# The front of a three-block network on one core: order of the loads, modulation products in four column quarters, and four of 31 convolution taps on TensorE

## The chip, the cores and the metric

The kernel runs on one core of a Trainium2 chip. The metric is the device time of one execution in microseconds; the time before is the median of three runs, 2841.48 us (2841.01 to 2846.5).

## What is computed

The reference chains two transformer-like layers over 512 latent and 256 context tokens of width 1024 and a third block over the latent tokens. Only the beginning matters here: the modulation vectors, the first norm, and the "conformer" convolution of the first layer.

```python
sc, scc = silu(c), silu(c_ctx)                       # 1024 each
mod_lat = sc @ ada_w[i] + ada_b[i]                   # i = 0, 1; 6 x 1024 columns each
mod_ctx = scc @ ada_w[i] + ada_b[i]                  # split in sh1, sc1, g1, sh2, sc2, g2
a = rmsnorm(h, norm1_g[0]) * (1 + sc1) + sh1         # 768 tokens x 1024
def conformer_conv(h, ...):
    u = h @ w_pw1 + b_pw1                            # 1024 -> 2048
    a, g = split(u, 2)
    v = a * sigmoid(g)
    v = dwconv(v, w_dw, b_dw)                        # depthwise, 31 taps over the tokens
    v = silu(layernorm(v, ln_g, ln_b))
    return v @ w_pw2 + b_pw2
h = h + g1 * conformer_conv(a, ...)
```

Everything is float32. `ada_w` is 2 x 1024 x 6144, some 50 MB, and is read once.

## The kernel before

Activations lie transposed: channels on the 128 partitions, tokens along the free axis, so a [1024, 768] activation is eight tiles k of 128 x 768. Each engine has its own hand-written program; they meet by counting semaphores, and each engine executes its own in order.

**Weights.** A 1024 x 128 piece of a weight matrix is a chunk. SyncE loads it into `raw` (two slots), ScalarE rounds it into `w_hi` (`high`, L520), GpSimd computes the rest `w_lo` = raw - w_hi (L490), and TensorE forms hi x hi, lo x hi and hi x lo (`tile_products`, L548 to L550). `high` for step i of a stream treats chunk i+2, after the products of chunk i. SyncE reloads a slot after `w_lo` of the chunk before in it.

**Start.** SyncE loads the constants, some 40 small parameter rows, then the token rows `x_rows` (L637, L638) and the first chunks of `pw1` (`raw`, L662). ScalarE first issues the eight 1 MB pieces of `ada_w` for the first 2048 modulation columns (`ada_x`, `ada_tail`, L645). TensorE transposes parameters (L695) and then token rows (L706); ScalarE copies them to `prm` and `h` (L711 to L720) and takes `silu(c)` to `sc`. Then norm `n10`: squares on ScalarE (L887), sums on VectorE (L896), sum over channels by a product with ones (L867), root (L1018), reciprocal (L1046).

**Modulation.** One piece of `ada_w` is 1024 x 256 (1 MB), its product is eight matmuls with 2 stationary columns (the two conditions) and 256 moving columns (L730). Four pieces make a group, which ScalarE copies out of PSUM (L757) and stores to a scratch in DRAM (L760). The first two groups are read back transposed (L768), turned (L747) and give shift and scale of `n10`. The other 40 pieces (n = 0 to 39) go through a ring of four buffers (`ada_tail`, `ada_s`); the load of piece n (L651) waits until piece n-4 is used.

**pw1 and convolution.** `pw1` has 16 chunks. For channel tile j (0 to 7), chunk 2j gives a (into PSUM pair j%2), chunk 2j+1 gives the gate half (pair 2). On TensorE: chunk 2j, chunk 2j+1, then six pieces of modulation (four for j=6, none for j=7). ScalarE, for steps i = 2j and 2j+1: `high` of chunk i+2, a modulation group if one is due, and in odd steps the sigmoid `gate` of tile j (L1160) and then `copy_conv` of tile j-1 to `cv` (L1175). VectorE: v = (a + b) * gate into `vp` (L1125), tap 0 (L1139), 30 more taps that accumulate in PSUM pair j%2 (L1142), each in two pieces of 512 and 256 tokens. TensorE may write chunk 2j+2 only when `copy_conv` of tile j-1 is done (`evac`), since both use the same PSUM pair.

SyncE's order of loads in this stage is written out in `pw1_sp`, and the change leaves it as it is:

```python
with sp.Fori(0, 2) as it:
    for u in range(4):
        w(it + 1, u)
        for n in range(3 * u - 3, 3 * u + 3) if u % 2 else ():
            ada_load(sp, it + 1, n, 1, ...)
```

So the two chunks of tile j+1 are requested after the last `ada_load` of tile j; that one waits until the second piece of tile j is used.

**Layer norm.** `mean_pe` (L1186) sums the eight `cv` tiles over channels with ones, `mean_dve` centres them (L1194), then squares, variance, norm and `pw2`.

Of the kernel before, what the change touches and what calls it, by code (L numbers as in the profile page):

```python
# [6 lines left out]
P = 128  # L7
D = 1024
KD = D // P
# [8 lines left out]
PAD = TAPS // 2  # L18
EPS = 1e-6
# [121 lines left out]
class Program:  # L141


    def __init__(self, nc, ctx, A):
# [22 lines left out]
        self.raw = at("raw", region(2 * w), [2, HALF * P])  # L167
        self.w_hi = at("w_hi", region(2 * w), [2, HALF * P], F32R)
        self.w_lo = at("w_lo", region(2 * w), [2, HALF * P], F32R)
# [5 lines left out]
        self.sc = at("sc", region(16 * 4), [2 * KD])  # L175
# [167 lines left out]
def build_in(nc, ctx, A, out, stop):  # L343
# [4 lines left out]

    s_cst = sem("s_cst", False)
# [3 lines left out]
    s_mod = sem("s_mod", False)  # L353
# [30 lines left out]
    cv_cent = sem("cv_cent")  # L384
    mu_ready = sem("mu_ready")
# [229 lines left out]
    def start_sp(sp):  # L615
        sp.dma_start(M.kb[:, :], A["k_base"]).then_inc(s_cst, 16)
# [20 lines left out]
        sp.dma_start(M.x_rows[:, 0:4, :], A["x"][0].rearrange("(t p) d -> p t d", p=P)).then_inc(s_rows, 16)  # L637
        sp.dma_start(M.x_rows[:, 4:6, :], A["ctx"][0].rearrange("(t p) d -> p t d", p=P)).then_inc(s_rows, 16)  # L638

    cond = M.sc[:, :].rearrange("p (s k) -> p k s", s=2)  # L640
    ada_src = A["ada_w"].rearrange("l (kt p) c -> p l kt c", p=P)

# [47 lines left out]

    def start_pe(pe):
        pe.wait_ge(s_cst, 16 * M.n_param_dma)
        for t in range(PT):
            bank = t // 4
            mm = pe.transpose(M.ps[:, bank * 512 + (t % 4) * P:bank * 512 + (t % 4 + 1) * P],  # L695
                              M.p_rows[:, t, :], ident)
            if t % 4 == 3 or t == PT - 1:
                mm.then_inc(start_t, 1)
        pe.wait_ge(s_rows, 32)
        for k in range(KD):  # L700

            pair = (k + 2) % 3
            if k >= 1:
                pe.wait_ge(start_c, done(k + 1))
            for t in range(6):
                mm = pe.transpose(M.pair(pair, t * P, (t + 1) * P), M.x_rows[:, t, k * P:(k + 1) * P], ident)  # L706
            mm.then_inc(start_t, 1)

    def start_act(act):
        act.wait_ge(start_t, done(1))  # L710
        act.activation(M.prm[:, 0:512], M.ps[:, 0:512], ACT.Copy).then_inc(start_c, 1)  # L711
        act.wait_ge(start_t, done(2))
        act.activation(M.prm[:, 512:1024], M.ps[:, 512:1024], ACT.Copy).then_inc(start_c, 1)
        act.wait_ge(start_t, done(3))
        act.activation(M.prm[:, 1024:PT * P], M.ps[:, 1024:PT * P], ACT.Copy).then_inc(start_c, 1)
        act.wait_ge(start_c, done(3))
        act.activation(M.sc[:, :], M.prm[:, COL["c"]:COL["c"] + 16], ACT.Silu).then_inc(sc_ready, 1)
        for k in range(KD):
            act.wait_ge(start_t, done(4 + k))
            act.activation(M.h[:, k, :], M.pair((k + 2) % 3), ACT.Copy).then_inc(start_c, 1)  # L720
# [5 lines left out]

    def ada_products(pe, weights, n):
        c = n // 4
        for k in range(KD):
            mm = pe.matmul(M.ps[32 * c:32 * c + 2, 3 * 1024 + (n % 4) * 256:3 * 1024 + (n % 4 + 1) * 256],  # L730
                           cond[:, k, :], weights[:, k, :], start=(k == 0), stop=(k == KD - 1),
                           tile_position=(0, 32 * c))
        mm.then_inc(ada_used, 1)

    def ada_pe(pe):
        pe.wait_ge(sc_ready, done(1))
        for n in range(ADA_FIRST):
            pe.wait_ge(s_ada[n], 16)
            ada_products(pe, M.ada_first[n], n)
        turn_mods_pe(pe, 0)  # L740
# [9 lines left out]
    def group_act(act, g, layer, column):  # L750

        c = g if g < 2 else (g - 2) % 3
        act.wait_ge(ada_used, done(4 * g + 4))
        if g >= 2:
            act.wait_ge(s_mod, 16 * g)
        r = slice(32 * c, 32 * c + 2)
        act.activation(M.mod_rows[r, :], M.ps[r, 3 * 1024:4 * 1024], ACT.Copy).then_inc(mod_rows, 1)  # L757
        act.wait_ge(mod_rows, done(g + 1))
        at = layer * 6 * D + column
        act.dma_start(mod_dram[:, at:at + 1024], M.mod_rows[r, :]).then_inc(s_mod, 16)  # L760

    def mods_back_act(act, second):
        n = 96 if second else 16
        act.wait_ge(s_mod, 16 * (MOD_GROUPS if second else 2))
# [5 lines left out]

    def pw1_pe(pe):
        first_two(pe, "pw1", BOTH, "n10")
        for it, u in peeled_chunks(pe, 16):
            peeled = isinstance(it, int)
            if not (peeled and 4 * it + u < 2):
                products(pe, "pw1", it, u, BOTH)
# [3 lines left out]
            for n in range(3 * u - 3, 3 * u + 3) if not peeled or it < 3 else range(4 if u == 1 else 0):  # L780
                if n % 4 == 0:
                    pe.wait_ge(mod_rows, done(3 * it + n // 4))
                pe.wait_ge(s_ring[n % 4], 16 * (3 * it + n // 4 + 1))
                ada_products(pe, M.ada_ring[n % 4], n)
# [17 lines left out]
    def ada_dve(dve):  # L802
        dve.wait_ge(mod_t, done(1))
        dve.wait_ge(start_c, done(3))
# [39 lines left out]
    def norm_source(eng, name, k):  # L844
# [4 lines left out]
        if name == "n10":  # L849
            eng.wait_ge(start_c, done(3 + k + 1))  # L850
# [161 lines left out]
    def norm_act(act, name):  # L1012
# [7 lines left out]
        if name == "n10":  # L1020
            for g in (0, 1):
                group_act(act, g, 0, g * 1024)
            mods_back_act(act, 0)
            act.wait_ge(mod_ready, done(1))
# [42 lines left out]
    def count_param_dmas():  # L1067

        n = 1 + 2
# [45 lines left out]

    def pw1_dve(dve):
        q0 = Q0["pw1"]
        cw = COL["conv_w_dw"]
        for j in range(8):
            pair = j % 2  # L1120
            dve.wait_ge(tile_done, done(q0 + 2 * j + 2))
            dve.wait_ge(gate_ready, done(j + 1))
            dve.wait_ge(zero_ready, done(2))
            for t0, t1, at in ((0, SEQ, VLAT), (SEQ, TOK, VCTX)):
                ins = dve.scalar_tensor_tensor(out=M.vp[:, j, at:at + t1 - t0], in0=M.pair(pair, t0, t1),  # L1125
                                               scalar=M.col("conv_b_pw1", j), in1=M.gate[:, j % 2, t0:t1],
                                               op0=ALU.add, op1=ALU.mult)
            ins.then_inc(v_ready, 1)
            dve.wait_ge(v_ready, done(j + 1))


            for tap in range(TAPS):
                for n, (t0, t1, at) in enumerate(((0, SEQ, VLAT), (SEQ, TOK, VCTX))):
                    src = M.vp[:, j, at - PAD + tap:at - PAD + tap + t1 - t0]
                    w = M.prm[:, cw + tap * 8 + j:cw + tap * 8 + j + 1]
                    o = M.pair(pair, t0, t1)
                    step = 2 * (TAPS * j + tap) + n
                    if tap == 0:
                        ins = dve.tensor_scalar(o, src, w, M.col("conv_b_dw", j), ALU.mult, ALU.add)  # L1139
                    else:  # L1140
                        dve.wait_ge(tap_done, done(step - 1))
                        ins = dve.scalar_tensor_tensor(out=o, in0=src, scalar=w, in1=o, op0=ALU.mult, op1=ALU.add)  # L1142
                    ins.then_inc(tap_done, 1)

    def pw1_act(act):
        for i in range(16):
            it, u = i // 4, i % 4
            high(act, "pw1", it, u)

            for g in range(10):  # L1150
                if group_step(g) == i:
                    layer, column = ((0, 2048 + g * 1024) if g < 3 else (1, (g - 3) * 1024) if g < 9 else (0, 5 * D))
                    group_act(act, g + 2, layer, column)
            if u % 2 == 0:
                continue
# [16 lines left out]
    def copy_conv(act, j):  # L1172
        pair = j % 2
        act.wait_ge(tap_done, done(2 * TAPS * (j + 1)))
        act.activation(M.cv[:, j, :], M.pair(pair), ACT.Copy).then_inc(cv_ready, 1)  # L1175
# [3 lines left out]
    def mean_pe(pe):  # L1179

        pair = Q0["pw2"] % 4
        pe.wait_ge(evac, done(Q0["pw2"]))
        for k in range(KD):
            pe.wait_ge(cv_ready, done(k + 1))
            for t0, tn in BOTH:
                mm = pe.matmul(M.pair(pair, t0, t0 + tn), ones, M.cv[:, k, t0:t0 + tn],  # L1186
                               start=(k == 0), stop=(k == KD - 1))
        mm.then_inc(mu_ready, 1)

# [1216 lines left out]
    def rw_dve(dve):  # L2406
# [80 lines left out]
        dve.wait_ge(zero_ready, done(3))  # L2487
# [39 lines left out]
    def _(pool):  # L2527
        prime(pool, [P_S.sem, lo_ready, zero_ready])
# [7 lines left out]
        if "pw1" in order:  # L2536
            pool.wait_ge(start_c, done(3 + KD))
            pool.memset(M.vp[:, :, :], 0.0).then_inc(zero_ready, 1)
        for name in used_streams:
# [8 lines left out]
            low_stream(pool, name)  # L2548

    @block.scalar  # L2550
    def _(act):
        prime(act, [mod_rows, hi_ready, start_c, sc_ready, sq_ready, rms_ready, y_ready, gate_ready, cv_ready,
                    mid_ready, silu_ready, ghi_ready, f_res, mem_ready, MIX.high, MIX.sq, MEMO.high, MEMO.sq, FFN2.high, FFN2.sq, mix_sd,
                    ffn2_sd, turn_c, fr_ready, q_hi, att_p, att_ea, att_h, S_S.sem])
        ada_first_load(act)
        act.wait_ge(zero_ready, done(1))
        start_act(act)
        if q_end:
            high_first(act)
# [39 lines left out]
    def _(pe):  # L2599
        prime(pe, [mod_t, tile_done, ada_used, start_t, stat_ready, mu_ready, mem_t, out_t, mix_stat, ffn2_stat, rope_r, turn_t, att_s, att_t, att_o, T_S.sem])  # L2600
# [112 lines left out]
```

## Time and profile before

| what | value |
|---|---|
| median of three runs | 2841.48 us |
| the profiled execution's own time | 2844.45 us |
| its span | 2842.7 us |
| TensorE, share busy | 88% |
| VectorE, share busy | 47% |
| first product of pw1 starts | 101.12 us |
| first v starts | 139.4 us |
| last tap ends, `cv` copied | 436.09 to 436.9 us |
| mean over channels done | 449.2 us |

Times in the trace count from the start of the span. A share of busy time says little here: what counts is, at each moment, which engine or load the others wait for. Only the first 482 us of the program are touched by the change; the rest follows unchanged.

### The profile page before, as it was taken

How to read it: one execution, taken by the hardware profiler on the slowest of the kernel's cores; microseconds unless marked ns; L12 is line 12 of the kernel's file. 1: busy time of each engine (PE TensorE's matmuls, PEld its weight loads, DVE VectorE, ACT ScalarE, POOL GpSimd, SP SyncE). 2: the span in 40 equal slices, each digit the busy share in tenths (PEclk: the TensorE clock that was granted, in tenths of full speed). 3: DMA queues.
4: the chain of work that ended last, by engine and by line, in shares of the span. 5: the costliest groups of instructions: out<-in, count | busy, mean ns of one | idle time of the engine just before them, and what ended most of it. 6: DMA issues, size and time to landing. Idle time of an engine off the chain costs nothing.

```text
span 2842.7 us, 33833 instructions
## 1 busy us (share of the span) xinstructions
PE 2508.0 (88%) x12581; PEld 1958.1 (69%) x12581; DVE 1347.9 (47%) x2245; ACT 925.4 (33%) x1385; POOL 706.3 (25%) x313
## 2 busy tenths in 40 slices
PE   3799944799999999799989999998965998999999
PEld 2456623688888888577767788776424887777877
DVE  2298896344313333648653223545455543542342
ACT  2311204443312322445444334433323211443341
POOL 1000100222222222210033444433001221344343
PEclk8999977899999999899989999999556987999999
DMA  5455600212212221210023333233000000333332
GB/s 195 136 184 169 208 24 1 59 52 66 66 53 65 61 66 58 62 43 1 10 88 89 96 90 102 83 105 93 1 0 1 1 1 0 89 89 96 89 94 91
DMA packets 336972, 204.53 MB, mean 72 GB/s; under 512 B 5846, under 2 KB 335040, under 8 KB 336728
## 3 DMA queue, kind: packets, MB, share of 16 engines
q1 hardware_dynamic: 326475, 190.88, 22.4%
q10 hardware_dynamic: 10380, 12.09, 1.3%
q8 instruction: 75, 1.23, 0.2%
q14 instruction: 42, 0.34, 0.0%
HBM read 200.74 MB, written 2.20 MB: 71 GB/s over the span
## 4 chain that ended last, share of the span: by engine, by line
PE 45%; issue 30%; POOL 10%; DVE 9%; ACT 2%; DMA 2%; DVEq 1%; SPq 1%; ACTq 0%; POOLq 0%
PE ps L548 10%; POOL w_lo L490 10%; PE ps L549 10%; PE ps L550 10%; PE ps L730 4%; DVE ps L1142 3%; PE ps L1379 2%; PE ps L2258 1%; PE ps L1407 1%; PE ps L2256 1%; PE ps L2248 1%; DMA raw<-in_conv_w_pw 1%; PE ps L1394 1%; DVE n_t L896 1%; DMA x_rows<-in_ctx 1%
## 5 line engine op out<-in xcount | busy, mean ns | idle before, releaser
L490 POOL TENSOR_TENSOR w_lo<-raw,w_hi 128x1024 fp32r<-128x1024 f32 (+1 forms) x253 | 646.3, 2557 | 1728.1 <-ACT w_hi L520 1727.8
L548 PE MATMUL ps<-x_hi,w_hi 128*128 128x512 f32 (+1 forms) x1864 | 678.0, 364 | 72.9 <-DVE x_lo L1053 47.5
L549 PE MATMUL ps<-x_lo,w_hi 128*128 128x512 f32 (+1 forms) x1864 | 667.2, 358 | 0.0
L550 PE MATMUL ps<-x_hi,w_lo 128*128 128x512 f32 (+1 forms) x1864 | 666.4, 358 | 0.0
L520 ACT ACTIVATE w_hi<-raw 128x1024 fp32r<-128x1024 f32 (+1 forms) x251 | 281.1, 1120 | 992.3 <-PE ps L550 797.4
L548 PEld LDWEIGHTS ps<-x_hi,w_hi 128*128 128x128 f32 x1864 | 355.9, 191 | 147.2 <-issue 68.5
L549 PEld LDWEIGHTS ps<-x_lo,w_hi 128*128 128x128 f32 x1864 | 356.7, 191 | 51.4 <-issue 2.6
L550 PEld LDWEIGHTS ps<-x_hi,w_lo 128*128 128x128 f32 x1864 | 355.7, 191 | 51.5
L1281 DVE SCALAR_TENSOR_TENSOR f_a<-ps,prm,f_a 128x511 f32<-128x511 f32 (+2 forms) x176 | 116.1, 681 | 374.8 <-ACT f_b L1247 363.9
L548 PE MATMUL ps<-g_hi,w_hi 128*128 128x512 f32 (+1 forms) x704 | 259.2, 368 | 14.7 <-DVE g_lo L1290 10.3
L549 PE MATMUL ps<-g_lo,w_hi 128*128 128x512 f32 (+1 forms) x704 | 257.3, 366 | 0.0
L550 PE MATMUL ps<-g_hi,w_lo 128*128 128x512 f32 (+1 forms) x704 | 257.2, 365 | 0.0
L1142 DVE SCALAR_TENSOR_TENSOR ps<-vp,prm,ps 128x512 f32<-128x512 f32 x480 | 252.7, 617 | 0.0
L548 PEld LDWEIGHTS ps<-g_hi,w_hi 128*128 128x128 f32 x704 | 134.7, 191 | 39.1 <-DVE g_lo L1290 12.9
L548 PE MATMUL ps<-xg_hi,w_hi 128*128 128x512 f32 x352 | 139.4, 396 | 12.2 <-POOL w_lo L490 12.2
L550 PEld LDWEIGHTS ps<-g_hi,w_lo 128*128 128x128 f32 x704 | 134.5, 191 | 21.0
L549 PEld LDWEIGHTS ps<-g_lo,w_hi 128*128 128x128 f32 x704 | 134.8, 191 | 20.3
L550 PE MATMUL ps<-xg_hi,w_lo 128*128 128x512 f32 x352 | 137.7, 391 | 0.0
L549 PE MATMUL ps<-xg_lo,w_hi 128*128 128x512 f32 x352 | 137.6, 391 | 0.0
L1313 DVE SCALAR_TENSOR_TENSOR h<-ps,mods,h 128x512 f32<-128x512 f32 (+1 forms) x48 | 30.3, 659 | 199.8 <-PE ps L550 199.8
L1251 ACT ACTIVATE ps<-f_a 128x512 f32<-128x512 f32 (+1 forms) x66 | 44.4, 673 | 222.5 <-DVE f_b L1281 222.5
L1281 DVE SCALAR_TENSOR_TENSOR f_b<-ps,prm,f_b 128x511 f32<-128x511 f32 (+2 forms) x176 | 115.0, 674 | 0.0
(315 smaller groups left out, 3203.0 us busy)
## 6 DMA issues: line engine op xcount, KB each, us to landing
raw<-in_ffn_w_up SPq DMA_DIRECT2D x88, 512.0 KB, 3.8
raw<-in_ffn_w_down SPq DMA_DIRECT2D x32, 704.0 KB, 4.5
raw<-in_w_up SPq DMA_DIRECT2D x44, 512.0 KB, 3.8
ada_tail<-in_ada_w SPq DMA_DIRECT2D x20, 1024.0 KB, 5.7
ada_s<-in_ada_w SPq DMA_DIRECT2D x20, 1024.0 KB, 7.5
raw<-in_conv_w_pw SPq DMA_DIRECT2D x24, 512.0 KB, 6.5
raw<-in_w_down SPq DMA_DIRECT2D x16, 704.0 KB, 4.4
raw<-in_w_in SPq DMA_DIRECT2D x17, 512.0 KB, 4.0
```

Of the source, the lines that this page charges most:

```text
L490: pool.tensor_tensor(M.w_lo[:, slot, 0:K * P], M.raw[:, slot, 0:K * P], M.w_hi[:, slot, 0:K * P].bitcast(F32), ALU.subtract).then_inc(lo_r ...
L520: act.activation(M.w_hi[:, slot, 0:K * P], M.raw[:, slot, 0:K * P], ACT.Copy).then_inc(hi_ready, 1)
L548: pe.matmul(o, wh, hi[:, k, t0:t0 + tn], start=(k == 0), stop=False)
L549: pe.matmul(o, wh, lo[:, k, t0:t0 + tn], start=False, stop=False)
L550: return pe.matmul(o, wl, hi[:, k, t0:t0 + tn], start=False, stop=(k == K - 1))
L730: mm = pe.matmul(M.ps[32 * c:32 * c + 2, 3 * 1024 + (n % 4) * 256:3 * 1024 + (n % 4 + 1) * 256], cond[:, k, :], weights[:, k, :], start=(k ...
L896: dve.tensor_tensor(M.n_t[:, 0, 0:w], M.n_sq[:, k % 2, 0:w], M.n_t[:, 0, 0:w], ALU.add).then_inc(sq_used, 1)
L1142: ins = dve.scalar_tensor_tensor(out=o, in0=src, scalar=w, in1=o, op0=ALU.mult, op1=ALU.add)
L1251: act.activation(M.pair(pa, 0, w), M.f_a[:, slot, 0:w], ACT.Silu).then_inc(silu_ready, 1)
L1281: ins = dve.scalar_tensor_tensor(out=dst[:, slot, o0:o1], in0=M.pair(pr, o0 + sh, o1 + sh), scalar=ffn_cols(b, tap, t, hf, j), in1=dst[:, ...
L1313: dve.scalar_tensor_tensor(out=o, in0=src, scalar=M.mods[:, 48 * b + 40 + m, s:s + 1], in1=o, op0=ALU.mult, op1=ALU.add)
L1379: mm = pe.matmul(M.pair(u % 2, off, off + n), lhs, rhs, start=first, stop=True, skip_group_check=True)
```

## The change

1. `rows_load`: ScalarE issues the two loads of the token rows ahead of the eight pieces of `ada_w`. TensorE turns token rows first, parameters after; ScalarE copies `h` first, then `prm`, then silu. The rounding of the first two chunks (`high_first`) moves from before the squares to behind the read-back of the first modulation vectors.
2. `ada_products`: takes two pieces at once (512 columns) as four quarters of 128 columns. Each quarter is a matmul with 32 stationary columns (the two conditions, padded with zeros) at `tile_position=(0, 32 * q)`. Eight k times four q, 128 moving columns each. A group's result lies in [128, 256] of PSUM, its store to the scratch is four small DMAs instead of one. Groups alternate between four places in PSUM. On ScalarE a group comes ahead of `high` in its step.
3. Four taps (0 to 3) of each tile are matmuls of `vp` with a diagonal matrix (`taps_pe`, float32), the other 27 stay on VectorE and accumulate onto them; GpSimd makes the diagonals. The bias goes into `copy_conv`. `taps_pe(j)` stands on TensorE behind tile j's modulation; v of tile j+1 (`gated(j + 1)`) now stands in VectorE's program inside the taps of tile j, ahead of the tap with index 18 of 27.
4. GpSimd sums `cv` tiles 0 to 6, `mean_pe` multiplies ones with the sum and with tile 7.

The core of the diff:

```diff
+    def rows_load(act):
+        act.dma_start(M.x_rows[:, 0:4, :], A["x"][0].rearrange("(t p) d -> p t d", p=P)).then_inc(s_rows, 16)
+        act.dma_start(M.x_rows[:, 4:6, :], A["ctx"][0].rearrange("(t p) d -> p t d", p=P)).then_inc(s_rows, 16)
...
     def start_act(act):
         for k in range(KD):
+            act.wait_ge(start_t, done(k + 1))
+            act.activation(M.h[:, k, :], M.pair(k % 3), ACT.Copy).then_inc(start_c, 1)
+        for n, bank in enumerate(PRM_BANKS):
+            act.wait_ge(start_t, done(KD + n + 1))
...
     def ada_products(pe, weights, n):
-        c = n // 4
+        g = n // 4
+        if n % 4 == 0 and g >= 2:
+            pe.wait_ge(mod_rows, done(g - 1))
+        at = mods_at(g) + n % 4 // 2 * P
         for k in range(KD):
-            mm = pe.matmul(M.ps[32 * c:32 * c + 2, 3 * 1024 + (n % 4) * 256:3 * 1024 + (n % 4 + 1) * 256],
-                           cond[:, k, :], weights[:, k, :], start=(k == 0), stop=(k == KD - 1),
-                           tile_position=(0, 32 * c))
-        mm.then_inc(ada_used, 1)
+            for q in range(4):
+                mm = pe.matmul(M.ps[32 * q:32 * q + 32, at:at + P], M.sc32[:, k, :],
+                               weights[q // 2][:, k, q % 2 * P:(q % 2 + 1) * P], start=(k == 0), stop=(k == KD - 1),
+                               tile_position=(0, 32 * q))
+        mm.then_inc(ada_used, 2)
...
+    def taps_pe(pe, j):
+
+        pe.wait_ge(v_ready, done(j + 1))
+        pe.wait_ge(diag_ready, done(j + 1))
+        for tap in range(PE_TAPS):
+            for t0, t1, at in ((0, SEQ, VLAT), (SEQ, TOK, VCTX)):
+                mm = pe.matmul(M.pair(j % 2, t0, t1), M.diag[j % 2][tap],
+                               M.vp[:, j, at - PAD + tap:at - PAD + tap + t1 - t0], start=(tap == 0),
+                               stop=(tap == PE_TAPS - 1))
+        mm.then_inc(pe_taps, 1)
...
     def pw1_pe(pe):
         first_two(pe, "pw1", BOTH, "n10")
+        for i in range(16):
+            it, u = i // 4, i % 4
+            if i >= 2:
                 products(pe, "pw1", it, u, BOTH)
             if u % 2 == 0:
                 continue
+            for n in range(12 * it + 3 * u - 3, min(12 * it + 3 * u + 3, 40), 2):
+                for m in (n, n + 1):
+                    pe.wait_ge(s_ring[m % 4], 16 * (m // 4 + 1))
+                ada_products(pe, M.ada_ring[n % 4:n % 4 + 2], ADA_FIRST + n)
+            taps_pe(pe, i // 2)
...
+        dve.wait_ge(zero_ready, done(3))
+        gated(0)
+        for j in range(8):
             dve.wait_ge(v_ready, done(j + 1))
+            dve.wait_ge(pe_taps, done(j + 1))
+            for i in range(DVE_TAPS):
+                if i == NEXT_AT and j < 7:
+                    gated(j + 1)
...
     def mean_pe(pe):
...
+        pe.wait_ge(cv_sum, done(6))
+        for t0, t1, half in ((0, 384, 0), (384, SEQ, 1), (SEQ, TOK, 1)):
+            pe.matmul(M.pair(pair, t0, t1), ones, M.cv_sum[:, half, t0 - 384 * half:t1 - 384 * half], start=t0 != 384,
+                      stop=False, skip_group_check=True)
+        pe.wait_ge(cv_ready, done(KD))
+        for t0, tn in BOTH:
+            mm = pe.matmul(M.pair(pair, t0, t0 + tn), ones, M.cv[:, KD - 1, t0:t0 + tn], start=False, stop=True,
+                           skip_group_check=True)
...
+    def pw1_pool(pool):
+        pool.wait_ge(start_c, done(3 + KD))
+        for j in range(8):
+            diag_pool(pool, j)
+            low_stream(pool, "pw1", 2 * j, 2 * j + 2)
+            cv_sum_pool(pool, j - 2)
+        low_stream(pool, "pw2", 0, 2)
+        cv_sum_pool(pool, 6)
+        low_stream(pool, "pw2", 2, 8)
```

## Rows read from the trace of the kernel before

**Rows 1.** Chain that ended last, pieces in time: start us, us, what.

```profile
59.25 27.93 PE ps L730 x128
...
96.75 0.97 DVE n_t L1057
...
121.37 19.95 PE ps L730 x96
...
158.19 19.96 PE ps L730 x96
...
334.43 1.15 DVE vp L1125 x2
...
336.87 30.54 DVE ps L1142 x59
...
436.09 0.82 ACT cv L1175
437.04 12.17 PE ps L1186 x32
```

**Rows 2.** A wait of ScalarE from 101 to 340 us: total us, times, longest.

```profile
ACT w_hi L520 <- DMA raw<-in_conv_w_pw: 179.1, 6, 33.0
```

**Rows 3.** Timeline of the start: start us, us, engine, line, idle before and releaser.

```profile
15.71 13.91 ACTq L645 DMA_DIRECT2D ada_tail<-in_ada_w  x2
43.32 0.87 ACT L887 ACTIVATE n_t<-h 128x768 f32<-128x768 f32 x1
44.95 3.08 DVE L896 TENSOR_TENSOR n_t<-n_sq,n_t 128x768 f32<-128x768 f32 x3 [44.95 <-ACT n_sq L887]
47.29 5.97 POOL L490 TENSOR_TENSOR w_lo<-raw,w_hi 128x1024 fp32r<-128x1024 f32 x2
48.27 7.93 DVE L896 TENSOR_TENSOR n_t<-n_sq,n_t 128x768 f32<-128x768 f32 x4 [0.23 <-ACT n_sq L887]
56.35 2.90 PE L867 MATMUL ps<-n_t,kb 128*128 128x512 f32 x4 [15.81 <-DVE n_t L896]
```

**Rows 4.** ScalarE's queue up to 29.65 us: packets, MB moved.

```profile
q10 hardware_dynamic: 6105, 6.17, 65.4%
```

**Rows 5.** SyncE's issues in the timeline, tile 1 of pw1.

```profile
161.77 3.82 SPq L651 DMA_DIRECT2D ada_s<-in_ada_w  x2
165.98 1.58 SPq L662 DMA_DIRECT2D raw<-in_conv_w_pw  x2
```

**Rows 6.** ScalarE in the timeline, tile 0, and tile 1's gate and copies.

```profile
137.11 1.28 ACT L1160 ACT_TABLE_LOAD   x1
...
172.33 1.06 ACT L520 ACTIVATE w_hi<-raw 128x1024 fp32r<-128x1024 f32 x1 [33.02 <-DMA raw<-in_conv_w_pw]
175.62 0.88 ACT L1160 ACTIVATE gate<-ps,prm 128x768 f32<-128x768 f32 x1
368.40 0.81 ACT L1175 ACTIVATE cv<-ps 128x768 f32<-128x768 f32 x1 [12.29 <-DVE ps L1142]
```

**Rows 7.** Issue to landing in us, min/median/max: pieces in ada_s; chunks of pw1.

```profile
DMA to landing us min/median/max: 5.1/7.5/9.0
DMA to landing us min/median/max: 3.9/7.3/21.9
```

**Rows 8.** TensorE's timeline: products into alternating column halves, and products over all columns.

```profile
2283.83 0.34 PE L2299 MATMUL ps<-u,tok 128*64 128x64 f32 x4
2283.95 0.34 PE L2301 MATMUL ps<-tok 128*64 128x64 f32 x4
```

**Rows 9.** TensorE's timeline: two idle times of 2.9 us; chunk 12 starts.

```profile
201.88 7.07 PE L730 MATMUL ps<-ada_s,sc 128*2 128x256 f32 x32
211.82 8.60 PE L730 MATMUL ps<-ada_tail,sc 128*2 128x256 f32 x32 [2.87 <-ACT mod_rows L757]
335.71 0.50 PE L548 MATMUL ps<-x_hi,w_hi 128*128 128x512 f32 x1
369.44 0.47 PE L548 MATMUL ps<-x_hi,w_hi 128*128 128x512 f32 x1 [2.88 <-ACTq L1177]
```

More of the change, by code:

```diff
@@ L18 @@
 PAD = TAPS // 2
+PE_TAPS = 4
 EPS = 1e-6
@@ L166, in __init__ @@
         w = HALF * P * 4
-        self.raw = at("raw", region(2 * w), [2, HALF * P])
-        self.w_hi = at("w_hi", region(2 * w), [2, HALF * P], F32R)
-        self.w_lo = at("w_lo", region(2 * w), [2, HALF * P], F32R)
+        r_raw, r_whi = region(2 * w), region(2 * w)
+        self.raw = at("raw", r_raw, [2, HALF * P])
+        self.w_hi = at("w_hi", r_whi, [2, HALF * P], F32R)
+        r_wlo = region(2 * w)
+        self.w_lo = at("w_lo", r_wlo, [2, HALF * P], F32R)
+        self.cv_sum = at("cv_sum", r_wlo, [2, HALF * P])[:, :, KD * P:HALF * P]
+        behind_8 = KD * P * 4
+        self.sc32 = at("sc32", r_whi + behind_8, [KD, 32])
+        diag = [at(f"diag{i}", r_raw + i * w + behind_8, [3, P]) for i in (0, 1)]
+        more = at("diag_more", r_whi + w + behind_8, [3, P])
+        self.diag = [[diag[i][:, n, :] for n in range(3)] + [more[:, i, :]] for i in (0, 1)]
         self.prm = at("prm", region(PT * P * 4), [PT * P])
@@ L352, in build_in @@
     s_ada = [sem(f"s_ada{i}", False) for i in range(ADA_FIRST)]
-    s_mod = sem("s_mod", False)
+    s_mod = [sem(f"s_mod{i}", False) for i in range(4)]
     s_modt = sem("s_modt", False)
@@ L384, in build_in @@
     cv_cent = sem("cv_cent")
+    diag_ready = sem("diag_ready")
+    pe_taps = sem("pe_taps")
+    cv_sum = sem("cv_sum")
     mu_ready = sem("mu_ready")
@@ L689, in pw1_sp @@
             w(3, u)
+    PRM_BANKS = (6, 7, 4)
     def start_pe(pe):
+        pe.wait_ge(s_kb, 16)
+        pe.wait_ge(s_rows, 32)
+        for k in range(KD):
+            if k >= 3:
+                pe.wait_ge(start_c, done(k - 2))
+            for t in range(6):
+                mm = pe.transpose(M.pair(k % 3, t * P, (t + 1) * P), M.x_rows[:, t, k * P:(k + 1) * P], ident)
+            mm.then_inc(start_t, 1)
         pe.wait_ge(s_cst, 16 * M.n_param_dma)
         for t in range(PT):
-            bank = t // 4
@@ L709, in start_act @@
[L709 to L720, printed above, removed]
+            act.wait_ge(start_t, done(k + 1))
@@ L1023, in norm_act @@
             mods_back_act(act, 0)
+            high_first(act)
             act.wait_ge(mod_ready, done(1))
@@ L1135, in pw1_dve @@
                     w = M.prm[:, cw + tap * 8 + j:cw + tap * 8 + j + 1]
[L1136 to L1140, printed above, removed]
+                    o = M.pair(j % 2, t0, t1)
+                    step = 2 * (DVE_TAPS * j + i) + n
+                    if i:
                         dve.wait_ge(tap_done, done(step - 1))
-                        ins = dve.scalar_tensor_tensor(out=o, in0=src, scalar=w, in1=o, op0=ALU.mult, op1=ALU.add)
-                    ins.then_inc(tap_done, 1)
+                    dve.scalar_tensor_tensor(out=o, in0=src, scalar=w, in1=o, op0=ALU.mult, op1=ALU.add)\
+                        .then_inc(tap_done, 1)
     def pw1_act(act):
@@ L1153, in pw1_act @@
                     group_act(act, g + 2, layer, column)
+            high(act, "pw1", it, u)
             if u % 2 == 0:
@@ L1181, in mean_pe, with diag_pool, cv_sum_pool, halves @@
         pair = Q0["pw2"] % 4
[L1182 to L1187, printed above, removed]
-        mm.then_inc(mu_ready, 1)
+        pe.wait_ge(evac, done(Q0["pw2"] - 4))
+        pe.wait_ge(cv_sum, done(6))
[6 more added lines that the diff above has]
+                           skip_group_check=True)
+        mm.then_inc(mu_ready, 1)
+    def diag_pool(pool, j):
+        if j >= 2:
+            pool.wait_ge(pe_taps, done(j - 1))
+        for tap in range(PE_TAPS):
+            c = COL["conv_w_dw"] + tap * 8 + j
+            ins = pool.tensor_scalar(M.diag[j % 2][tap], ident, M.prm[:, c:c + 1], None, ALU.mult)
+        ins.then_inc(diag_ready, 1)
+    def cv_sum_pool(pool, j):
+        def halves(k):
+            return M.cv[:, k, :].rearrange("p (a b) -> p a b", a=2)
+        if j < 1:
+            return
+        pool.wait_ge(cv_ready, done(j + 1))
+        if j == 1:
+            pool.tensor_tensor(M.cv_sum, halves(0), halves(1), ALU.add).then_inc(cv_sum, 1)
+            return
+        pool.wait_ge(cv_sum, done(j - 1))
+        pool.tensor_tensor(M.cv_sum, M.cv_sum, halves(j), ALU.add).then_inc(cv_sum, 1)
+    def pw1_pool(pool):
[7 more added lines that the diff above has]
+        low_stream(pool, "pw2", 2, 8)
     def mean_dve(dve):
@@ L2547, in _ @@
                 continue
-            low_stream(pool, name)
+            if name == "pw1":
+                pw1_pool(pool)
+            elif name != "pw2":
+                low_stream(pool, name)
     @block.scalar
```

96 lines of the change are left out of this document (46 added, 50 removed).

## The prediction

> **What bounds the kernel now.** I read four views. The page says TensorE is busy 88% of the time; that is a mean over the whole program and says nothing of the first 480 us, the only part the change touches. So the chain of waits comes first, cut to this part. The reader is to see in [rows 1] whose pieces follow each other: the first modulation product (27.93 us), a store and read-back through DRAM, then in the `pw1` stage TensorE's modulation (19.95 us per tile) alternating with its products until v of tile 5 at 334.43 us, and from there VectorE's taps without a gap to the last `cv` copy at 436.09, then the mean's 12.17 us. So TensorE sets the pace up to tile 5, VectorE after it. The waits of ScalarE come second: [rows 2] shows that it stands still for the load of `pw1` chunks six times, 179 us in all. Today that costs little, because TensorE is busy with modulation meanwhile. It is cover that the change takes away. Third, the timelines of SyncE and ScalarE around tile 1 [rows 5, 6] show why the load is late: chunk 3 ends at 158.19 [rows 1], the second piece of modulation is used 6.7 us later, and only then (165.98) does SyncE request the next two chunks; the first is rounded at 172.33, and the sigmoid, behind both roundings in ScalarE's program, comes at 175.62. Fourth, landing times and TensorE's clock [rows 7, 9].
>
> **The start.** ScalarE's queue accepts the last piece of `ada_w` at 15.71 + 13.91 = 29.6 us [rows 3], when the queue has moved 6.17 MB [rows 4]. With 3.1 MB of token rows ahead in the same queue it is held longer: at that queue's mean of 6.17 MB in 27 us the rest would take 13.6 us, but the same bytes only change places between two queues that share the engines, so I take 4.4 us, until 34 (bounds 29.6 and 43.2). Behind it on ScalarE: a table load and eight copies of `h` (7.4), three copies of `prm` (1.5), table and silu (1.5), so the squares start at 44.4 instead of 43.32 [rows 3]. The early token rows therefore bring nothing; TensorE waits for ScalarE. `w_lo` no longer runs beside the sums: four additions took 7.93 us beside it, the three ahead of it 3.08, 1.03 each, so 3.8 us go. The ones product starts at 56.35 + 1.1 - 3.8 = 53.7 and ends 2.9 later.
>
> **Modulation.** One pass of 256 moving columns takes 27.93/128 = 0.218 us [rows 1], so one of 128 takes 0.109. A pair of pieces is 64 passes. Whether the quarters run at once is not shown by this kernel's modulation; the nearest row is the product into alternating 64-column halves: four passes of 64 columns every 0.12 us [rows 8], 0.03 each, where one alone should take 0.055. Two halves run at once there. Four quarters at once give 64 x 0.109/4 = 1.75 us; I take 1.9. Bounds: 1.75, and 7.0 for one after another. The Trainium skill ("TensorE: Matmul & The Clock Gate", "Why this matters for your kernels") gives 2.38 times for three column tiles; by it a pair costs 7.0/3.2 = 2.2 us, an estimate, and the sum would end some 3 us later. The halves' row agrees that tiles overlap.
>
> Four pairs 7.6, plus 1.0 because the clock is at half when they begin (the ones product's 2.90 us, [rows 3], is the half rate). Modulation ends at 53.7 + 2.9 + 8.6 = 65.2 against 59.25 + 27.93 = 87.2. From there to the first scaled tile (96.75) are 9.6 us: copy, store, read-back. Four DMA issues instead of one, 0.3 each, less 0.5 for a copy of 256 columns: 10.0. `high_first` (2.0) stands behind the read-back's issue and is hidden by its landing and the turn, some 3.5 us; without that cover it costs up to 2. So the first scaled tile comes at 75.2, 21.6 earlier, and chunk 1 ends at 121.37 - 21.6 = 99.8.
>
> **Tile 0.** Call A, B, C the three pairs of a tile. A ends at 101.7. SyncE requests C's two pieces and then chunk 3. Two pieces land 7.5 us after their issue, a chunk alone in 3.9, of which I count 1.9 as transfer [rows 7]: chunk 3 lands 9.6 after A, at 111.3. Rounding 1.1, table load 1.3, sigmoid 0.9 [rows 6], v 1.15 [rows 1], handing over 0.1: 115.8 (139.4 + 1.15 before). `taps_pe(0)` then: four taps of 768 columns at four passes' cost, 3 x 2 x 0.218 = 1.3 us each, 5.2 in all, and 7.1 as TensorE has idled 4 us and begins at half clock. VectorE's taps and chunk 2 start at 122.9; before, chunk 2 started at 121.37 + 19.95 = 141.3. 18.4 us gained.
>
> **The cycle of tiles 1 to 5.** Here the change adds a wait. v of tile j now stands inside VectorE's taps of tile j-1, nine taps from their end; those nine, the `copy_conv` behind them, and by `evac` TensorE's chunk 2j+2 all queue behind it. v waits for the sigmoid, that for the roundings, these for the chunks that SyncE requests after A. So the ring is closed:
>
> - two chunks on TensorE, from 121.37 + 19.95 = 141.32 to 158.19 [rows 1]: 16.9
> - A: 1.9 (6.7 before)
> - two pieces and two chunks land: 0.25 + 7.5 + 2 x 1.9 = 11.5 (before 172.33 - 164.9 = 7.4 for the first, one piece having gone ahead). Bounds 10 and 13.5
> - rounding 1.1, sigmoid 0.9, v 1.15, handing over: 3.2
> - nine taps at 2 x 30.54/59 = 1.035 us [rows 1]: 9.3
> - to the next chunk: 369.44 - 368.37, the copy [rows 6] and its signal: 1.1
>
> The sum is 43.9 us a tile. B, C and `taps_pe(j)` lie in its cover: C lands about 8 after A, the four taps end some 7 after v, under the nine. Tiles 2 and 4 have a group's copy and four issues between the two roundings, 1.2 each. Before each new chunk TensorE idles 3 us; an idle time of 2.9 once cost 8.60 - 7.07 = 1.5 us of clock and once nothing [rows 9], so 0.8 each. Five cycles: 5 x 44.7 + 2.4 = 226, to 349. Before, the same five took 335.7 [rows 9] - 141.3 = 194. The 18.4 us gained become 13 lost.
>
> **The end.** For tile 6 the chunks are requested early (only four pieces, none after), so the cycle is 16.9 + 3.2 + 9.3 + 1.1 = 30.5: chunk 14 at 379.5, tile 6's taps end at 409, and tile 7's 27 x 1.035 = 28.0 end at 437. Before it was 436: the shorter VectorE work (four taps, 4.1 us a tile less) has only made up for the cycle. The mean keeps one tile behind the last copy: at half clock 2.9 [rows 3] instead of 12.17, so 9.3 less. GpSimd's sums and diagonals fill its idle time; if `cv_sum` of tile 6 were late (some 2 us of work after 409) it would still be 25 us early. In the tap rows, which read PSUM and one SBUF operand, no slowing beside GpSimd's `w_lo` is seen; the Trainium skill ("GPSIMD Engine Reference", "Key points") limits the contention to instructions with two SBUF inputs or a two-port mode, and the additions in [rows 3] agree.
>
> Sum: the last copy 1.3 us later, the mean 9.3 shorter: 8 us off. The profiled 2844.45 would be 2836.5; it stands 3 above the median of the runs, so I predict 2834. Smaller than 0.2%, 5.7 us, this kernel's measurement does not tell from no change.
>
> **Rivals.**
> - *The weights are hidden* (0.06): if the chunks were there when asked for, five cycles would be 30.5 as for tile 6, some 67 us less: 2767. The intended saving on VectorE would show in full. [rows 2] and the unchanged request order speak against it.
> - *A better start* (0.09): ScalarE free at 29.6 as before, roundings fully covered, clock up earlier: 12 us less, 2822.
> - *Quarters overlap only with their neighbour* (0.10): if a pass of the next quarter starts only when both passes of the one before have started, two run at a time: 64 x 0.109/2 = 3.5 a pair, 1.6 more for four pairs at the start and six A's: 16 us, 2850, slower. It decides once a pair costs over 3.0. The halves' four passes in 0.12 us speak against it, as they too come four in one half, then four in the other. The skill's first-named page ("Step-by-step: what each phase is for") says that matmuls stay in program order, which would give this.
> - *No overlap* (0.05): 7.0 a pair, 5.1 x 10: 2885.
> - *The forecast* (0.70): 2834, its own range 2818 to 2852. Over five cycles the landing's bounds give -7 to +10, the start's -4 to +9 (where ScalarE is held until 43), the clock +-4. Of it 0.40 is faster, 0.18 the same, 0.12 slower.
>
> Faster 0.40 + 0.06 + 0.09 = 0.55; same 0.18 + 0.02 of the neighbour case = 0.20; slower 0.12 + 0.08 + 0.05 = 0.25. The range 2806 to 2853 leaves out the first and the fourth rival and thin tails.
>
> **What would show it.** A pair of modulation near 1.9 us; the squares starting near 44 and the first scaled tile near 75; 44 us between chunk 2j starts for tiles 1 to 5, then 30; VectorE idle some 14 us a tile ahead of v, released by the sigmoid, and ScalarE waiting for `raw` before it; the last tap within 5 us of 436; the mean 3 us after the copy. Cycles near 30, or pairs over 3 us, would make it wrong.

## The result, and the profile after

The median went from 2841.48 us to 2849.69 us (twelve runs each, 2840.57 to 2847.16 before and 2841.48 to 2853.21 after). The ratio is 1.0022 with a 95% interval of 1.0015 to 1.003: slower, by 8.2 us at the medians. The kernel before was run again beside the experiments, with medians from 2841.28 to 2843.29; against these the loss is 6.4 to 8.4 us. Forecast were 2834 us and, with a chance of 0.55, a gain. The time lies inside the range, on the wrong side of no change.

The profiled execution took 2853.21 us, its span is 2851.1, 8.4 more than before. The chain of waits shows where they go. First its longest pieces (start us, us, what); lines 757, 560, 1192, 1225 and 1239 of the changed kernel are 730, 548, 1142, 1175 and 1186 of the kernel before.

```profile
54.30 2.90 PE ps L908 x4
57.20 8.66 PE ps L757 x256
...
99.94 1.93 PE ps L757 x64
...
116.15 8.14 PE ps L808 x16
140.94 1.93 PE ps L757 x64
...
145.81 9.00 DMA raw<-in_conv_w_pw
154.84 1.06 ACT w_hi L532
155.89 0.80 ACT gate L1210
156.78 1.14 DVE vp L1169 x2
157.93 8.47 DVE ps L1192 x17
...
167.42 0.91 ACT cv L1225
187.09 1.93 PE ps L757 x64
...
449.65 0.91 ACT cv L1225
450.60 2.94 PE ps L1239 x4
```

Against [rows 1]: the first modulation ends at 65.9 instead of 87.2, chunk 1 at 99.9 instead of 121.4. 21.4 us are gained. Then a period of seven pieces repeats: a modulation pair, the load of the next weights, rounding, sigmoid, v, taps, copy, and after it the next chunks. A load of 9 us stands in the chain once for each of tiles 1 to 5 (and once in tile 0). In the chain before, a load stood in three places in all, and no taps or copy behind it before tile 5:

```profile
202.83 6.74 DMA raw<-in_conv_w_pw
281.91 6.18 DMA raw<-in_conv_w_pw
323.58 6.57 DMA raw<-in_conv_w_pw
```

The last copy is 13.6 us later than before; the mean, 2.94 instead of 12.17, gives 9.2 back.

The waits of VectorE, TensorE and ScalarE from 101 to 440 us (total us, times, longest), first two of the kernel before, then the changed one:

```profile
DVE vp L1125 <- ACT gate L1160: 23.6, 1, 23.6
...
ACT w_hi L520 <- DMA raw<-in_conv_w_pw: 190.3, 7, 33.0
```

```profile
DVE vp L1169 <- ACT gate L1210: 110.9, 8, 20.6
...
PE ps L560 <- ACTq L1227: 22.0, 6, 5.1
PE ps L757 <- DMA ada_s<-in_ada_w: 21.8, 4, 7.0
PE ps L757 <- ACT mod_rows L784: 21.3, 2, 10.7
PE ps L808 <- DVE vp L1169: 16.8, 7, 3.4
...
ACT w_hi L532 <- DMA raw<-in_conv_w_pw: 182.0, 11, 38.1
```

ScalarE waits for the weights about as long as before in this stretch (182 us against 190), but now VectorE waits 111 us for the sigmoid behind them, where it waited 24 us before, and TensorE waits in its turn for the copy that VectorE's taps hold up (22 us).

### The profile page after: what moved, and what is told of

Its sections match the earlier page's. It is cut to its first block, busy times and chain, and to the rows that moved or that the text cites. A ratio compares the mean times of both kernels' runs of the same rounds, so it can differ in the third digit from the quotient of the medians.

```text
span 2851.1 us, 35564 instructions
## 1 busy us (share of the span) xinstructions
PE 2460.1 (86%) x13455; PEld 1981.8 (70%) x13455; DVE 1311.7 (46%) x2181; ACT 918.3 (32%) x1385; POOL 736.3 (26%) x352
## 4 chain that ended last, share of the span: by engine, by line
PE 43%; issue 30%; POOL 10%; DVE 9%; ACT 3%; DMA 2%; ACTq 2%; DVEq 1%; SPq 0%; POOLq 0%
PE ps L560 11%; PE ps L561 10%; PE ps L562 10%; POOL w_lo L502 9%; DVE ps L1192 3%; PE ps L1463 2%; DMA raw<-in_conv_w_pw 2%; PE ps L2342 1%; ACTq L658 1%; PE ps L1491 1%; PE ps L2340 1%; PE ps L2332 1%; PE ps L757 1%; PE ps L1478 1%; DVE n_t L937 1%
## 5 line engine op out<-in xcount | busy, mean ns | idle before, releaser
L560 PE MATMUL ps<-g_hi,w_hi 128*128 128x512 f32 (+1 forms) x704 | 259.0, 368 | 14.7 <-DVE g_lo L1374 10.3
L1192 DVE SCALAR_TENSOR_TENSOR ps<-vp,prm,ps 128x512 f32<-128x512 f32 (+1 forms) x432 | 227.5, 615 | 8.3 <-PE ps L808 8.3
L1335 ACT ACTIVATE ps<-f_a 128x512 f32<-128x512 f32 (+1 forms) x66 | 44.4, 673 | 222.5 <-DVE f_b L1365 222.5
```

Source lines behind the costliest of these rows:

```text
L560: pe.matmul(o, wh, hi[:, k, t0:t0 + tn], start=(k == 0), stop=False)
L1335: act.activation(M.pair(pa, 0, w), M.f_a[:, slot, 0:w], ACT.Silu).then_inc(silu_ready, 1)
```

## The experiments

In the changed kernel chunk 2j starts 1.1 us after the copy of tile j-2 (from tile 2 on), so the distance of two copies is the length of a tile. Tile 1 takes 44.3 us in the changed kernel, tiles 2 to 5 take 47.6, 46.3, 48.9 and 46.9.

**The load out of the ring.** SyncE requests the chunks of tile j+1 before the pieces that wait for tile j's first pair:

```diff
-        with sp.Fori(0, 2) as it:
-            for u in range(4):
-                w(it + 1, u)
-                for n in range(3 * u - 3, 3 * u + 3) if u % 2 else ():
-                    ada_load(sp, it + 1, n, 1, sp.snap(it * (12 * 256) + n * 256))
...
+        for t in range(1, 7):
+            for n in range(6 * t, 6 * t + 4):
+                ring(n)
+            for i in (2 * t + 2, 2 * t + 3):
+                w(i // 4, i % 4)
+            if t < 6:
+                ring(6 * t + 4)
+                ring(6 * t + 5)
```

> The changed kernel, but SyncE requests the two chunks of tile j+1 ahead of the last two modulation pieces of tile j (and chunk 3 ahead of the last two of tile 0), so that no chunk waits for modulation to be used. Theory A (the five long tiles are a closed ring of chunk products, first modulation pair, load of the next chunks, sigmoid, v, nine taps, copy): without the load in the ring the next bound is the third modulation pair, 16.9 + 1.9 + 8.3 + 1.9 + 5.2 = 34 us a tile instead of 46.8, so about 60 us less than the changed kernel, near 2787. Theory B (the loads are covered; the tiles are long because TensorE has more to do at a lower clock): less than 10 us of difference.

Measured: 2795.03 us, ratio to before 0.9834 (0.9818 to 0.9851), 54.7 us less than the changed kernel. From copy to copy five tiles take 35.7 to 37.7 us; theory A said 34. Most of the difference is clock: the third pair, behind its wait, took 3.3 us at a granted clock of 0.57 and 3.6 at 0.50 instead of 1.93. The chunks, behind the taps without an idle time, took 16.7. VectorE's first wait is now the one that theory A named next, the four taps behind the third pair and its load (waits, total us, times, longest):

```profile
DVE ps L1196 <- PE ps L812: 49.1, 6, 12.3
DVE vp L1173 <- ACT gate L1214: 17.4, 2, 13.4
```

**Where v stands among the taps.** One number changed, in both directions:

```diff
-    NEXT_AT = 18
+    NEXT_AT = 24        # the other run: 9
```

> The changed kernel with v of the next tile ahead of the tap with index 24 of 27 instead of 18, so three taps lie behind it instead of nine. Theory A: for the tiles that wait for the sigmoid the copy comes 6.2 us earlier, but then TensorE's own four taps (6.5 to 8 us behind v) are the next bound, so some 3 us less a tile, plus the clock that the idle time ahead of the chunk cost (1.5 to 2.5); tiles 6 and 7, where v came without a wait, get longer by 3 to 4 each. Together 8 to 18 us less than the changed kernel, 2832 to 2842. Theory B (v's place does not matter, the tile is bound by TensorE's work): within 3 us of the changed kernel for the first five tiles.

> The changed kernel with v ahead of the tap with index 9, so eighteen taps lie behind it. Theory A: every tile from 1 to 7 grows by nine taps, 9.3 us, 65 us together, near 2915. Theory B: no change, as VectorE's order would be hidden under TensorE.

Measured: 2827.91 us with v at 24 (ratio 0.9943, 0.9924 to 0.9963) and 2919.85 us with v at 9 (1.0267, 1.0248 to 1.0287). Nine taps more behind v cost 70 us at the medians, and the last copy comes 65.2 us later (514.85 us), which is seven tiles at 9.3: the taps behind v are paid in full. With six taps fewer behind v, tiles 1 to 5 are 39 to 43 us long instead of 44 to 49. The gain, 22 us, is above the upper end of what was expected (18): TensorE starts its chunks right behind its taps, and they took 16.7 us at a granted clock of 1.00. Theory B is out.

**The taps back on VectorE.** v stands at the head of its tile again, all 31 taps behind it:

```diff
-        gated(0)
         for j in range(8):
+            gated(j)
             dve.wait_ge(v_ready, done(j + 1))
-            dve.wait_ge(pe_taps, done(j + 1))
-            for i in range(DVE_TAPS):
-                if i == NEXT_AT and j < 7:
-                    gated(j + 1)
+            for tap in range(TAPS):
...
-            taps_pe(pe, i // 2)
...
-            diag_pool(pool, j)
```

> The changed kernel with its third part taken back: all 31 taps on VectorE, v at the head of its tile, no diagonal products and no diagonals; start, quarters and GpSimd's sums stay. Theory A: nothing queues behind v but its own tile, the ring is chunks 17 to 19, pair 1.9, load and sigmoid 14, v and the copy 2, some 36 to 37.5 us, close to VectorE's own 33.9; from the first v at 116 the last copy comes near 400 instead of 450, so about 49 us less than the changed kernel, near 2801, although VectorE does more. Theory B (taps on VectorE are what limits): slower than the changed kernel by up to 8 x 4.1 = 33 us.

Measured: 2790.08 us, ratio 0.9818 (0.9801 to 0.9834): 59.6 us less than the changed kernel, 51.6 less than before, with 33 us more work on VectorE. So the start, the quarters and the mean alone are worth 51.6 us, and the taps on TensorE together with v inside its neighbour's taps, as the change places them, cost all of it and 8 more. This run takes back both at once; the two runs before it show what v's place does by itself. VectorE's waits fall from 111 to 26.5 us, in the first the start's 21.6, and the last copy comes at 391.27 instead of 449.65:

```profile
DVE vp L1168 <- ACT gate L1207: 26.5, 4, 21.6
```

```profile
391.27 0.81 ACT L1222 ACTIVATE cv<-ps 128x768 f32<-128x768 f32 x1 [33.03 <-DVE ps L1189]
```

**The order of requests in the kernel before**, the same edit as in the first experiment:

> The kernel before, with only the order of SyncE's requests changed as in the run with the weights first. Theory A (before, the late request is covered by TensorE's 20 us of modulation a tile, save for two or three stalls of 5 us): 5 to 11 us less than before, 2831 to 2836. Theory B (the order of requests is a fault of its own, and what it brought in the changed kernel has nothing to do with the quarters and the taps): 40 us or more less.

Measured: 2820.72 us, ratio 0.9917 (0.9903 to 0.9932), 21 us less than the first median before and 23 less than the one beside it (2843.29). Neither number: half of it I had overlooked. The first sigmoid comes at 128.9 instead of 138.4, as it too stood behind a load (of chunk 3); and the first four tiles from copy to copy take 35.2 to 38.3 us instead of 37.1 to 42.2. The late request cost 21 to 23 us before the change already, and 55 with it; so 32 to 34 of the 55 are its interplay with the change.

**The third pair behind the four taps**, on top of the weights first:

```diff
+            n0 = 12 * it + 3 * u - 3
+            for n in range(n0, min(n0 + 6, 40), 2):
+                if n == n0 + 4:
+                    taps_pe(pe, i // 2)
                 for m in (n, n + 1):
                     pe.wait_ge(s_ring[m % 4], 16 * (m // 4 + 1))
                 ada_products(pe, M.ada_ring[n % 4:n % 4 + 2], ADA_FIRST + n)
-            taps_pe(pe, i // 2)
+            if n0 + 4 >= 40:
+                taps_pe(pe, i // 2)
```

> The changed kernel with the weights first, and with the third modulation pair of each tile behind the tile's four taps on TensorE. Theory A: in the run with the weights first, VectorE waited 49 us in six waits for the four taps, which stood behind the third pair and its load. With the pair behind them the tile is 16.9 + 1.1 + 0.9 + 1.2 to v, nine taps and the copy, 30.6 instead of 36 to 38, and tile 0 some 6 us shorter: 30 to 35 us less than that run, 2760 to 2766. Theory B (TensorE's four taps are themselves too slow at a low clock): less than 10 us.

Measured: 2766.94 us, ratio 0.9732 (0.9718 to 0.9746), 28.1 us less than with the weights first alone and a little under the 30 to 35 expected; the last copy comes 33.4 us earlier (362.84 against 396.22). From copy to copy a tile takes 30.7 us four times, 32.2 and 32.3 once each. The 49.1 us of waiting for TensorE's taps have shrunk to one wait of 7.3.

**All taps on VectorE, and the weights first**, the two edits together:

> All 31 taps on VectorE and the weights first. Theory A: VectorE alone then sets the pace, 33.9 us a tile from a first v at 107 instead of 115: last copy at 379 instead of 391, 2778. So the four taps on TensorE, with everything in the right order, should be worth 12 to 18 us, not 33, since each tile keeps 1.6 us of waiting and starts with TensorE's taps. Rival: still 2790, if the load of the weights was no part of its 33.8 us tiles.

Measured: 2774.91 us, ratio 0.9759 (0.9745 to 0.9773); tiles of 33.8 us, VectorE's own work. So with everything in order the four taps on TensorE are worth 2774.9 - 2766.9 = 8 us at the medians of four runs each, less than the 12 to 18 expected. In the profiled executions, though, the last copy comes 16.6 us earlier with them (362.84 against 379.43), and the spans are 15.3 us apart. The profiled execution with the taps was the fastest of its four (2759.62 us, the others 2766.6 to 2768.9); where those three lost 7 to 9 us no trace shows. The taps give 8 to 17 us, a quarter to a half of the 33 us of work that they take off VectorE.

**Idle products against the fall of the clock.** The result of the added products is read by nobody.

```diff
             taps_pe(pe, i // 2)
+            for _ in range(5):
+                pe.matmul(M.pair(2, TOK, 1024), ident, M.vp[:, i // 2, 0:256], start=True, stop=True,
+                          skip_group_check=True)
```

> The changed kernel with five idle products on TensorE behind each tile's four taps (the identity times 256 columns of v, into 256 columns of PSUM that nothing reads; 2.1 us at full clock), in the 2.8 to 3.5 us in which it idles before the next tile's chunks. Theory A (the two chunks of tiles 2 to 5 and 7 took 18.6 to 19.7 us instead of 16.9 because the clock had fallen in that idle time): 16.9 again, the clock at 1.0 in these stretches, five cycles of 226 instead of 234 and 8 to 13 us less, near 2839. Theory B (the additional time is not the clock's): no change, or 1 to 2 us more where the idle products are in the way.

Measured: 2846.54 us, ratio 1.0008 (0.9999 to 1.0017), some 3 us less than the changed kernel, not 8 to 13. The stretches from the first product of chunk 2j to its tile's modulation show why; first of the changed kernel, for tiles 1 to 7, then of this one, for tiles 2 to 6 (columns: stretch, length, TensorE busy, granted clock, share of DMA, GB/s):

```profile
124.30:141.00 16.70, 16.70 (x100) 1.00 0.00 1
168.40:187.10 18.70, 18.55 (x100) 0.91 0.01 1
216.00:234.70 18.70, 18.54 (x100) 0.91 0.00 0
262.40:282.20 19.80, 19.72 (x100) 0.85 0.01 1
311.30:330.60 19.30, 19.22 (x100) 0.87 0.01 1
358.30:375.20 16.90, 16.90 (x100) 1.00 0.13 37
389.00:408.70 19.70, 19.62 (x96) 0.85 0.09 27
```

```profile
171.60:188.50 16.90, 16.82 (x96) 1.00 0.01 1
217.80:234.60 16.80, 16.74 (x96) 1.00 0.01 1
262.50:279.30 16.80, 16.80 (x96) 1.00 0.01 1
309.00:328.50 19.50, 19.48 (x96) 0.84 0.01 1
356.30:373.20 16.90, 16.83 (x96) 1.00 0.15 41
```

Where the clock was at 1.0 the chunks took 16.9 us, where it was partly at 0.5 up to 19.8. In the changed kernel TensorE had idled 2.8 to 5.1 us ahead of the slow chunks of tiles 2 to 5 and 7, and 2.1 ahead of tile 6's, which ran at full clock. The idle products restored the clock in three of tiles 2 to 5; in the fourth, tile 5, TensorE still idled 3.0 us behind them, as it also did ahead of tile 3's, where the clock stayed up. This shortened the way from the first copy to the last from 282.2 to 275.9 us. But in tile 0, where no idle time follows the taps, the products stood in the way for 2.2 us, and the first copy came 3.1 later. Theory A names the cause of the longer chunks, its size of 8 to 13 us was too high.

**A plain delay in the kernel before.** The results of the added instructions are not used.

```diff
         dve.wait_ge(mu_ready, done(1))
+        for _ in range(4):
+            dve.tensor_tensor(M.n_t[:, 1, :], M.cv[:, 0, :], M.cv[:, 1, :], ALU.add)
+            dve.drain()
```

> The kernel before with four idle additions of 0.97 us on VectorE (results unused) between the mean and the centring, a plain delay of 4.0 to 4.4 us on the path and nothing else. The changed kernel was 4.3 us late at this place and 8.4 at the end, though everything behind it is the same code. Theory A (the rest is lost where TensorE idles now and then and its clock falls by chance of timing): 4 to 9 us more than before, with the additional part in the attention and recurrence stages, and more spread between runs. Theory B (something of the change acts on the later stages): 4.0 to 4.4 exactly.

Measured: 2844.97 us, ratio 1.001 (1.0001 to 1.0018), 12 runs from 2843.01 to 2849.87. The four additions took 4.07 us, and the median is 1.7 us above the one beside it. The interval reaches from 0.3 to 5.1 us, so the medians don't decide between the two expectations. The traces say more: the profiled execution is still 4.1 us late at 1960 us, yet its span is only 0.4 us longer than before. In this pair of executions the code behind gave the delay back. The place shows in a stretch of the third block, the same work in the kernel before (whose next stretch is shown too), the changed and the delayed one (the first five columns are the length and the busy time of TensorE, its weight loads, VectorE and ScalarE; the one behind GpSimd's is the granted clock):

```profile
2096.00:2142.00 46.00, 24.44 (x42) 10.76 (x41) 26.40 (x47) 11.78 (x20) 0.00 (x0) 0.61 0.00 0
2195.00:2240.00 45.00, 41.30 (x350) 39.11 (x349) 19.24 (x31) 8.08 (x18) 11.97 (x12) 0.92 0.01 1
```

```profile
2104.00:2145.00 41.00, 19.80 (x40) 8.53 (x39) 26.08 (x46) 11.61 (x18) 0.00 (x0) 0.66 0.00 0
2199.00:2248.00 49.00, 44.70 (x346) 42.32 (x345) 19.24 (x31) 8.08 (x18) 11.93 (x12) 0.85 0.00 1
```

```profile
2101.00:2143.00 42.00, 20.46 (x40) 8.77 (x41) 26.36 (x46) 11.62 (x19) 0.00 (x0) 0.65 0.00 0
```

In this stretch the changed kernel makes up 5 us, and in the next (2199 to 2248, clock 0.85 where the kernel before had 45 us at 0.92) it loses 4 again. The same instructions take some us more or less, with another granted clock; each kernel has one trace here, so what belongs to the kernel and what to the single execution stays open.

**A better start.** On top of the third pair last, SyncE issues four of the eight first pieces of `ada_w`:

```diff
-        for n in range(ADA_FIRST):
+        for n in range(4):
             act.dma_start(M.ada_first[n], ada_src[:, 0, :, n * 256:(n + 1) * 256]).then_inc(s_ada[n], 16)
...
         w(0, 1)
+        for n in range(4, ADA_FIRST):
+            sp.dma_start(M.ada_first[n], ada_src[:, 0, :, n * 256:(n + 1) * 256]).then_inc(s_ada[n], 16)
```

> The kernel with the third pair last, and the last four of the eight first modulation pieces issued by SyncE behind its first two chunks instead of by ScalarE. Theory A (the start is bound by ScalarE, whose own queue of loads holds it to 34.6 us): ScalarE is free by some 15 us, the squares start near 27 as soon as the parameters are in, the first modulation product waits for the last of the 8 MB near 42 and the first scaled tile comes near 55 to 60 instead of 75: 12 to 20 us less than the run with the third pair last, 2747 to 2755. Theory B (the start is bound by the bytes): less than 5 us.

Measured: 2750.71 us, ratio 0.9675 (0.9658 to 0.9691), 16.2 us less than with the third pair last, inside the expected 12 to 20: theory A. ScalarE is free at 18.6 us instead of 34.6 and its squares start at 29.43 instead of 45.23 (timeline of the changed kernel, then of this one):

```profile
26.03 8.51 ACTq L658 DMA_DIRECT2D ada_tail<-in_ada_w  x2
34.63 1.28 ACT L727 ACT_TABLE_LOAD   x1 [34.63 <-issue]
...
45.23 0.83 ACT L928 ACTIVATE n_t<-h 128x768 f32<-128x768 f32 x1
```

```profile
3.73 14.80 ACTq L658 DMA_DIRECT2D ada_x<-in_ada_w  x4
18.63 1.28 ACT L733 ACT_TABLE_LOAD   x1 [18.63 <-PE ps L719]
...
29.43 0.83 ACT L938 ACTIVATE n_t<-h 128x768 f32<-128x768 f32 x1
```

**And v at 20**, on top of that (`NEXT_AT = 20`):

> The run before of this list, with v at the tap with index 20. VectorE still waited some 1.7 us a tile for the sigmoid at 18 in the run with the third pair last, 12 us in seven waits. At 20 v should come without a wait and the seven taps behind it, 7.2 us, should still cover TensorE's four (5.2 to 6): 7 to 11 us less than at 18. If TensorE's taps run at the low clock (6.5 and more plus handing over) it is 3 us or less.

Measured: 2737.12 us, ratio 0.9623 (0.9605 to 0.964), 104 us less than before and the fastest kernel of this study. The last copy comes 6.3 us earlier than with v at 18 (341.14 against 347.44), just under the 7 to 11 expected. The medians are 13.6 us apart, four runs each, but the two profiled spans are alike (2742.5 and 2742.1); what makes up the other 7 us is not shown.

## Why the prediction was wrong

The structure of it held. The price of its ring of waits and the share of clock in it were too low, and the sum was a small difference of large terms. It said 8 us less, the profiled execution took 8.4 more: of the 16.4 between them 1.4 arose in tile 0, 8 in tiles 1 to 5, 2.8 in the last two tiles and 4.1 behind the front.

- **The start**: right. Squares at 45.23 (44.4 forecast), the ones product at 54.30 (53.7), first modulation 8.66 us (8.6), first scaled tile 75.3 (75.2), chunk 1's end 21.4 earlier (21.6).
- **Pairs of modulation**: right, 1.93 us (1.9) at full clock, against 19.95/3 = 6.65 before: 3.4 times for four column tiles. The estimate by the Trainium skill ("TensorE: Matmul & The Clock Gate", "Why this matters for your kernels"), 2.2 us, was further off than the one from the halves' row. The rival drawn from matmuls in program order, 3.5 us a pair, did not occur, nor did the one without overlap.
- **Tile 0**: v at 114.95 (114.65 forecast), but TensorE's four taps took 8.14 us, not 7.1, at a granted clock of 0.66; at 1.00 they took 5.4 in the run with the weights first. Chunk 2 starts 1.4 us late.
- **The cycle**: this step failed, in its clock term. Five cycles, chunk 2 at 124.3 to chunk 12 at 358.3, took 234 us; forecast were 226. What was mis-sized most is the 0.8 us of clock a tile: the chunks took 18.7 to 19.8 us at a granted clock of 0.85 to 0.91 in tiles 2 to 5, so 1.8 to 2.9 more than 16.9. Over the five tiles that is 8.7 us where the sum had 4, so 4.7 of the 8. The two idle times in [rows 9] were a sample of two. The run with idle products gave 6 us back, 5 of them in these tiles. Another 2.7 us lie between the first pair and v: v is done 15.0 to 15.2 us behind the pair in tiles 1, 3 and 5 (14.7), and 16.5 and 16.7 in tiles 2 and 4 (15.9), where a group's copy stands between the roundings. Taps and copy follow the list within 0.2 us a tile.
- **The end**: tile 6 as forecast (30.7 against 30.5), but tile 7's chunks took 2.8 us more at a granted clock of 0.85, a term that the sum put at nothing. With 1.4, 8 and this the taps end at 449.2 instead of 437. The mean gave its 9.2.
- **Behind the front** no term stood at all. The changed kernel is 4.3 us late when the mean is done and 8.4 at the end. In the delayed kernel 4.3 us at that place became 0.4 in the profiled execution and 1.7 at the median, so the rest doesn't pass a delay on as it is. Three of the changed kernel's twelve runs ended at 2841.5 to 2842.0, where the kernel before usually is. Whether 4 us are the change's due or chance is left open.
- **The rival of hidden weights** was priced wrong: I gave it 30.5 us a tile and 2767. With the weights out of the way (first experiment) the third pair's load takes over at 36 to 38, 2795. It needs both edits to come to 30.7 and, as it happens, 2767.

Above all the comparison hid the lesson. The prediction counted what the parts give against the kernel before and found them nearly cancelled; the runs show what they give by themselves: start, quarters and mean 51.6 us, four taps on TensorE 8 to 17 us when well placed, and minus 59.6 us as placed.

## What to carry to other kernels

When a long task is sped up, look for what was waiting in its shadow: here requests for weights stood, in an in-order queue, behind the use of other data, and 20 us of products a tile had hidden part of their price (the late request cost 21 to 23 us before, 55 after). An instruction whose input may come late must not stand inside a run of instructions that another engine needs: v, nine taps from the end of its neighbour's, turned a load that delayed its own tile into one that also held up the taps of the tile before and, through its copy, the next chunks. Where the input is there in time the same place does little harm: in the fastest kernel v stands in its neighbour's taps too, and waits 3.8 us in all behind tile 0. And undo each part of a bundle separately before judging any; the one that took 33 us of work off VectorE, the engine that set the pace of the last tiles, cost the most.

## What was not expected of the hardware

- Four column tiles of 32 stationary columns in float32, eight k times two passes each, ran 3.4 times as fast as the same products with 2 stationary and 256 moving columns, one after another (64 passes in 1.93 us, 30 ns each, against 6.65 us, both at a granted clock of 1.00).
- An engine that issues loads is held by its own queue: ScalarE stood until 34.6 us behind 11 MB of its own requests, and until 18.6 behind 7; the bytes moved in all were the same and the squares started 16 us earlier.
- A delay of 4.07 us on the path made the median 1.7 us higher (0.3 to 5.1), and the same stretch of later code took 46 us in one kernel and 41 in another. The last copy's time in the trace and the median of the whole differed by up to 9 us on what an edit is worth (16.6 against 8.0 for the four taps). A difference of the whole below that says little about the part that was edited; the copy's time says it for one execution.
